# A hybrid decoder layer on one core: other orders at the first pair, the late pairs and the last scalings

## The chip, the core and the metric

The kernel runs on one core of a Trainium2 chip. Time is device time in microseconds (us) from start to end of one execution. The core has a matmul engine (TensorE, in the profile PE, its weight loads PEld), three engines for elementwise work (VectorE = DVE, ScalarE = ACT, GpSimd = POOL) and SyncE (SP), which here issues nearly all DMAs. Every engine has its own instruction stream, executed in the order in which it is written; the streams meet only at semaphores.

## What is computed

One decoder layer over 1024 tokens of width 1024, in float32: modulation vectors from `c`; RMSNorm, one input projection, two groups of four heads of chunked linear attention with decay, each head normed and gated; an output projection and a residual; RMSNorm and a squared-ReLU MLP with a residual; a last RMSNorm with gain.

```python
mod = silu(c) @ w_ada + b_ada            # shift1, scale1, gate1, shift2, scale2, gate2
h = rms_norm(x) * (1 + scale1) + shift1
# per head, chunks of 64: scores inside the chunk, a state from chunk to chunk
o = chunk_gated_linear_attention(q, k, v, log_a, 64)
o = rms_norm(o, g) * silu(gate)          # o * exp(-0.5 * ln(mean(o*o) + eps))
x = x + gate1 * (concat(o) @ w_out)
h = rms_norm(x) * (1 + scale2) + shift2
x = x + gate2 * (square(relu(h @ w_mlp1)) @ w_mlp2)
return rms_norm(x, final_norm_g)
```

## The kernel before

Every large product is made in three passes of a rounded format: both operands are split into a high part (a rounding copy, on ACT) and a low part (the rest, on POOL or DVE), and PE adds high x high, high x low and low x high. One step is a matmul of 128x128 weights with 128x512 data.

The span falls into the first norm (to 40 us), three groups of input units with attention in between (to 224 us), eight *pairs* (224 to 440 us), the output projection (to 520 us), the MLP and, after 1130 us, the last norm. The change touches the pairs and the last norm.

**A pair** makes two column blocks of the input projection as a 2x2 block product with seven instead of eight half products: P1 to P7. Their weights are quarters of `w_in` (`pair_quarter`, loaded by SP in `load_pair_quarter`) and sums of quarters, made on DVE (`weight_sum_of`, S1 to S4; S3, S2, S1 and S4 feed P7, P6, P5 and P3). ACT rounds each (`pair_high`), POOL takes the low part (`pair_low`), PE multiplies (`pair_product`, 12 matmuls; P7 in four pieces of three matmuls, `seventh_piece`, whose right operand SP loads piece by piece as `piece_x` and `piece_y`). DVE adds the products to the four quarters of the result (`join` "11", "u", "22", "21", "12"; "u" is the sum that two of them share), after ACT has saved one product (`copy_part`). Each quarter lies in a bank that a later pair writes: `c_read[...]` counts the reads that free it. The first piece of a pair's P7 waits for `c_read["12"]` of the pair before, which `silu_of` "12" raises.

Two pairs make one head: the early one its queries and forget gate, the late one its output gate and values. `paired(gi, h)` runs for gi = 3, 4, 5 and `gates(6)` last; each has a version for each engine, and for PE it is `two_pairs`. Between the products PE does the attention of the head before, in steps (`attend(n)`): transposed keys `k`, state updates `up`, scores `sc`, outputs `o`, sums of squares `ss`, transposed values `v`. ACT's `output` copies an attention output and squares it, the squares are split (`sq_hi` on ACT, `sq_lo` in DVE's `low_squares`), `ss` sums them; `norm_log` and `norm_exp` (or `read_out` in the first three groups) make the inverse root; DVE multiplies it in (`norms`). ACT loads a table before a logarithm and again before an exponential. `far_keys` and `far_queries` on DVE scale half of the keys and of the queries by a chunk's decay, for scores that span two chunks.

At the first pair (p = 0) the group H0 ends: ACT's `read_out(7, "ss")` takes two logarithms and two exponentials of a head pair, DVE's `read_out(7)` norms (`normed`) and `gate` gates head 0. `piece_y` lies where the statistics of one of these heads lie, so SP's `load_piece(0, 1)` waits for `normed`. `high_fourth` and `low_fourth` split the fourth right operand, which P4 uses.

**The end.** PE transposes tile by tile of x back (`y_bank`). ACT sums squares and takes roots, DVE inverts (`root`), multiplies by gain and root (`last_norm`) into `out_stage`; some half tiles were multiplied by the gain alone before their root was known, and get the root later (`scale_left` on ACT, a loop at the end of POOL's stream, one operation in `last_norm(7)` on DVE). SP stores tile after tile. The last add to x runs in three parts on DVE (L3180, L3183, L3187); the third waits for PE's last product.

Of the kernel before, what the change touches and what calls it, by code (L numbers as in the profile page):

```python
# [25 lines left out]
ACT = mybir.ActivationFunctionType  # L26
# [264 lines left out]
def hybrid_layer(nc, x, c, w_ada, b_ada, w_in, gate_w2, gate_b2, gla_g, lb_logits, hgrn_g, w_out, w1, w2,  # L291
# [3 lines left out]
    with ExitStack() as ctx:  # L295
# [359 lines left out]
        def _(sp):  # L655
# [57 lines left out]
            def load_piece(p, j):  # L713
# [6 lines left out]
                if p == 0 and j == 1:  # L720
                    sp.wait_ge(normed, before("ss", 3))
# [200 lines left out]
            for t in range(TT - 1):  # L922
                sp.wait_ge(read["y"], 4 + 2 * (t + 1) if t < 4 else 13 + t - 4)
                if t in (3, 4, 5):
                    sp.wait_ge(scaled_x, 2 * KT + t - 2)
                if t in (3, 6):
                    sp.wait_ge(normalised, 2 * TT + t // 3)
                sp.dma_start(out[0, t * P:(t + 1) * P, :], out_stage[:, t, :]).then_inc(stored, 16)
            for j in (1, 0):
                sp.wait_ge(read["y"], 17 - j)  # L930
                sp.dma_start(out[0, D - P:D, j * HALF:(j + 1) * HALF],
                             out_stage[:, TT - 1, j * HALF:(j + 1) * HALF]).then_inc(stored, 16)
# [4 lines left out]
        def _(pool):  # L937
# [129 lines left out]
            for t, j in ((3, 1), (4, 0), (5, 0)):  # L1067
                cols_ = slice(j * HALF, (j + 1) * HALF)
                pool.wait_ge(read["y"], 4 + 7)
                pool.wait_ge(rms_ready, 2 + t + 1)  # L1070
                pool.tensor_scalar(out_stage[:, t, cols_], out_stage[:, t, cols_], fin[:, t, 3:4], None, ALU.mult
                                   ).then_inc(scaled_x, 1)
# [3 lines left out]
        def _(act):  # L1076
# [114 lines left out]
            def group(name, gi, h):  # L1191
# [135 lines left out]
                else:  # L1327
# [6 lines left out]
                    read_out(7, "ss")  # L1334
# [17 lines left out]
            def copies(gi):  # L1352
# [16 lines left out]
                def output(half):  # L1369

                    src = bank_of("o", half)
                    act.wait_ge(normed, before("o", gi) + half)
                    act.activation(stat[:, 0, :], src, ACT.Square).then_inc(o_squared, 1)
                    act.activation(tok(mixed[:, gi + 1], half), src, ACT.Copy).then_inc(read["o"], 1)
                    act.wait_ge(o_squared, before("o", gi) + half + 1)
                    act.activation(sq_hi[:, 0, :], stat[:, 0, :], ACT.Copy).then_inc(sq_hi_ready, 1)
# [38 lines left out]
            def paired(gi, h):  # L1415
# [9 lines left out]
                if early:  # L1425
                    pair_high(early, P6)
                wait_join(act, early, 0)
                keys(0)
                if not early:
                    pair_high(early, P6)  # L1430
                copy_part(early, 0)
                if not early:
                    high_fourth()
                pair_high(early, P5)
# [319 lines left out]
            for n, (t, j) in enumerate(Y_ORDER):  # L1754
# [19 lines left out]
                if (t, j) == (3, 1):  # L1774
                    scale_left(3)
            scale_left(6)


        @block.tensor
        def _(pe):  # L1780
# [312 lines left out]
            def two_pairs(name, gi):  # L2093
# [209 lines left out]
        def _(dve):  # L2303
# [210 lines left out]
            def group(name, gi, h):  # L2514
# [71 lines left out]
                def gate(u, n, head, half=None, place=None):  # L2586


                    th, xx = (t0[:, :], t1[:, :]) if half is None else (tok(t0, place), tok(t1, place))
                    for hf in (0, 1) if half is None else (half,):  # L2590
                        dve.wait_ge(unit_read[hf], u + 1)
                    dve.scalar_tensor_tensor(th, th, 1.0, xx, ALU.add, ALU.mult).then_inc(gate_silu, 1)
                    dve.wait_ge(gate_silu, n + 1)

# [733 lines left out]
```

## Time and profile before

| what | us |
|---|---|
| median of 3 runs (1162.1 to 1164.61) | 1164.46 |
| the profiled execution, own time | 1164.09 |
| its span, first to last instruction | 1162.3 |
| PE busy in the span | 1133.2 (97%) |
| DVE busy | 865.7 (74%) |
| ACT busy | 613.0 (53%) |
| POOL busy | 496.9 (43%) |

Times below count from the start of the profiled span. Busy time of PE is modelled and overlaps from matmul to matmul; distances between starts of matmuls show its pace. The granted clock of PE has a mean of 0.993 of full speed over the span; its levels here are 1.00 (2.4 GHz) and 0.50 (1.2 GHz).

### The profile page before, as it was taken

Reading aid. Unit: us, or ns where it says so; the run is one execution under the profiler, and the core shown is the slowest. Engines: PE = TensorE matmul, PEld = TensorE weight load, DVE = VectorE, ACT = ScalarE, POOL = GpSimd, SP = SyncE. Lnnn points to the kernel's source line nnn. Section 1 sums busy time; section 2 is a strip of 40 time slices with the busy share of each in tenths; the row PEclk is TensorE's granted clock in tenths of the full one; section 3 lists DMA queues with packets and bytes.
Section 4 is the critical chain, followed back from the end, with each engine's and each line's share of the span. In section 5 each row is a group of like instructions: output and inputs, shape, how many; then the busy total and the mean of one; then the engine's idle time right before and its main releaser. Section 6 shows DMA issues by size and latency. Waiting matters only on the chain.

```text
span 1162.3 us, 15518 instructions
## 1 busy us (share of the span) xinstructions
PE 1133.2 (97%) x5483; PEld 935.7 (81%) x5483; DVE 865.7 (74%) x1033; ACT 613.0 (53%) x933; POOL 496.9 (43%) x320
## 2 busy tenths in 40 slices
PE   7999999999999999999999999999999999999996
PEld 6788788777878788888888888888888888888885
DVE  6898887778677767377976765677795875966876
ACT  7763555757566566255654555455663533524424
POOL 1021122144343345427525353344466675666741
PEclk9999999989999999999999999999999999999998
DMA  9778387344353536721455344544624637437203
GB/s 359 260 235 271 129 210 203 77 127 123 101 168 106 151 104 227 239 90 75 140 167 182 136 155 135 181 143 160 190 63 161 227 91 262 162 128 275 69 2 145
DMA packets 162948, 186.71 MB, mean 161 GB/s; under 512 B 7604, under 2 KB 119352, under 8 KB 159928
## 3 DMA queue, kind: packets, MB, share of 16 engines
q1 hardware_dynamic: 160472, 179.44, 46.6%
q0 software_dynamic: 2400, 6.29, 2.8%
q8 instruction: 44, 0.72, 0.3%
q14 instruction: 32, 0.26, 0.1%
HBM read 138.51 MB, written 40.89 MB: 154 GB/s over the span
## 4 chain that ended last, share of the span: by engine, by line
PE 89%; DVE 3%; DMA 3%; ACT 2%; issue 1%; SPq 1%; POOL 0%; DVEq 0%; ACTq 0%
PE unit_bank L1782 19%; PE unit_bank L2220 9%; PE unit_bank L2221 9%; PE unit_bank L2222 9%; PE small_bank L2220 9%; PE small_bank L2221 9%; PE small_bank L2222 9%; PE small_bank L1782 4%; PE unit_bank L2067 3%; PE unit_bank L2069 3%; PE unit_bank L2068 3%; DMA ada_slot<-in_w_ada_dram 1%; PE small_bank L1821 1%; PE small_bank L1924 1%; DVE ada_acc L2321 1%
## 5 line engine op out<-in xcount | busy, mean ns | idle before, releaser
L1026 POOL TENSOR_TENSOR wr_lo<-quarter,wr_hi 128x512 fp32r<-128x512 f32 x122 | 198.1, 1635 | 174.2 <-ACT wr_hi L1570 174.1
L2220 PE MATMUL unit_bank<-op_hi,wr_hi 128*128 128x512 f32 x452 | 176.8, 391 | 0.2 <-issue 0.2
L2222 PE MATMUL unit_bank<-op_hi,wr_lo 128*128 128x512 f32 x452 | 176.2, 390 | 0.0
L2221 PE MATMUL unit_bank<-op_lo,wr_hi 128*128 128x512 f32 x452 | 176.1, 390 | 0.0
L2220 PE MATMUL small_bank<-op_hi,wr_hi 128*128 128x512 f32 x448 | 174.7, 390 | 0.0
L2221 PE MATMUL small_bank<-op_lo,wr_hi 128*128 128x512 f32 x448 | 174.5, 389 | 0.0
L2222 PE MATMUL small_bank<-op_hi,wr_lo 128*128 128x512 f32 x448 | 174.5, 389 | 0.0
L1570 ACT ACTIVATE wr_hi<-wr_full 128x512 fp32r<-128x512 f32 x90 | 56.8, 631 | 173.3 <-DVE wr_full L2986 165.6
L1570 ACT ACTIVATE wr_hi<-quarter 128x512 fp32r<-128x512 f32 x136 | 83.0, 626 | 90.2 <-PE unit_bank L2222 51.2
L2986 DVE TENSOR_TENSOR wr_full<-quarter,quarter 128x512 f32<-128x512 f32 x90 | 89.2, 992 | 55.4 <-PE small_bank L2222 23.7
L1782 PE MATMUL unit_bank<-a_hi,w_hi 128*128 128x512 f32 x304 | 121.2, 399 | 0.0
L1782 PE MATMUL unit_bank<-a_hi,w_lo 128*128 128x512 f32 x304 | 118.6, 390 | 0.0
L1782 PE MATMUL unit_bank<-a_lo,w_hi 128*128 128x512 f32 x304 | 118.6, 390 | 0.0
L1026 POOL TENSOR_TENSOR wr_lo<-wr_full,wr_hi 128x512 fp32r<-128x512 f32 x48 | 80.5, 1679 | 76.3 <-ACT wr_hi L1570 53.6
L2220 PEld LDWEIGHTS unit_bank<-op_hi,wr_hi 128*128 128x128 f32 x452 | 84.9, 188 | 18.7 <-issue 1.2
L2222 PEld LDWEIGHTS unit_bank<-op_hi,wr_lo 128*128 128x128 f32 x452 | 84.9, 188 | 17.7
L2221 PEld LDWEIGHTS unit_bank<-op_lo,wr_hi 128*128 128x128 f32 x452 | 84.9, 188 | 17.6 <-issue 0.2
L2220 PEld LDWEIGHTS small_bank<-op_hi,wr_hi 128*128 128x128 f32 x448 | 84.1, 188 | 17.5 <-POOL wr_lo L1026 0.2
L2222 PEld LDWEIGHTS small_bank<-op_hi,wr_lo 128*128 128x128 f32 x448 | 84.1, 188 | 17.6
L2221 PEld LDWEIGHTS small_bank<-op_lo,wr_hi 128*128 128x128 f32 x448 | 84.2, 188 | 17.2
L941 POOL TENSOR_TENSOR w_lo<-raw,w_hi 128x1024 fp32r<-128x1024 f32 x11 | 29.4, 2673 | 122.5 <-ACT w_hi L1083 122.5
L983 POOL TENSOR_TENSOR pw_lo<-pair_quarter,pw_hi 128x512 fp32r<-128x512 f32 x32 | 49.2, 1538 | 58.9 <-ACT pw_hi L1344 58.9
(382 smaller groups left out, 2368.0 us busy)
## 6 DMA issues: line engine op xcount, KB each, us to landing
quarter<-in_w_mlp_dram SPq DMA_DIRECT2D x128, 256.0 KB, 4.1
hidden_scratch<-hid SPq DMA_DIRECT2D x98, 256.0 KB, 2.3
ada_slot<-in_w_ada_dram SPq DMA_DIRECT2D x48, 512.0 KB, 6.7
op_full<-hidden_scratch SPq DMA_DIRECT2D x21, 1024.0 KB, 4.8
pair_quarter<-in_w_in_dram SPq DMA_DIRECT2D x32, 256.0 KB, 4.0
piece_x<-t_scratch SPq DMA_DIRECT2D x16, 512.0 KB, 4.1
piece_y<-t_scratch SPq DMA_DIRECT2D x32, 256.0 KB, 3.5
raw<-in_w_out_dram SPq DMA_DIRECT2D x16, 512.0 KB, 4.5
```

The source lines that it names most:

```text
L941: pool.tensor_tensor(w_lo[slot][:, :, :], raw[slot][:, :, :], w_hi[slot][:, :, :].bitcast(F32), ALU.subtract).then_inc(wlo_ready, 1)
L983: pool.tensor_tensor(pw_lo[place][:, :, :], pair_source(prod), pw_hi[place][:, :, :].bitcast(F32), ALU.subtract).then_inc(pair_lo, 1)
L1026: pool.tensor_tensor(wr_lo[slot][:, :, :], split_source(n), wr_hi[slot][:, :, :].bitcast(F32), ALU.subtract).then_inc(wr_lo_pool, 1)
L1570: act.activation(wr_hi[slot][:, :, :], split_source(n), ACT.Copy).then_inc(wr_hi_ready, 1)
L1782: return pe.matmul(out_ap, left, right, start=start, stop=stop)
L2067: pe.matmul(dst, wh, hi[:, k, :], start=k == 0 and prod not in (P6, P3), stop=False, skip_group_check=True)
L2068: pe.matmul(dst, wh, lo[:, k, :], start=False, stop=False, skip_group_check=True)
L2069: mm = pe.matmul(dst, wl, hi[:, k, :], start=False, stop=k == KH - 1, skip_group_check=True)
L2220: pe.matmul(dst, wh, ah, start=opens, stop=False, skip_group_check=True)
L2221: pe.matmul(dst, wh, al, start=False, stop=False, skip_group_check=True)
L2222: mm = pe.matmul(dst, wl, ah, start=False, stop=k == KH - 1, skip_group_check=True)
L2986: dve.tensor_tensor(dst[:, :, :], a[:, :, :], b[:, :, :], op).then_inc(w_sum, 1)
```

## The change

1. **First pair.** ACT: the two logarithms (`first_logs`) come first, then P6's rounding, the keys and the part's copy, then the exponentials (`first_exps`). They take the two heads in the other order. DVE: norm and gate of H0 (`first_norms`, `first_gate`) stand behind S1, `join` "11" and `states(0)`; `masks(0)` comes before `low_fourth`. PE: the scores (`attend(2)`) come before the seventh product's pieces 1 and 2. SP's load of `piece_y` waits for the first of the two norms instead of both.
2. **Late pairs of the three heads.** DVE: S4 right behind `join` "11", `low_squares(1)` before the queries, S2 and `join` "21" before `far_keys`, `join` "12" before `norms(1)`, `far_queries` behind S1 of the next pair. ACT: `value_of(0)` and the rounding of P7 and P2 come before `norm_log(1)` and `norm_exp(1)`; `output` writes the rounded squares first, straight from the bank, and then the full ones.
3. **Gates.** `low_squares(0)` before S2.
4. **End.** DVE takes both halves of tile 3 and the left half of tile 5, ACT those of tiles 6 and 7, POOL that of tile 4 alone. SP stores tile 4 in two halves and tile 7 in one piece.

On SP:

```diff
                 if p == 0 and j == 1:
-                    sp.wait_ge(normed, before("ss", 3))
+                    sp.wait_ge(normed, before("ss", 2) + 3)
...
+            sp.wait_ge(scaled_x, 2 * KT + 2)
+            store(3)
+            sp.wait_ge(read["y"], 4 + 9)
+            store(4, right)
+            sp.wait_ge(scaled_x, 2 * KT + 3)
+            store(4, left)
+            sp.wait_ge(read["y"], 4 + 11)
+            store(5)
+            sp.wait_ge(read["y"], 4 + 12)
+            sp.wait_ge(normalised, 2 * TT + 1)
+            store(6)
+            sp.wait_ge(read["y"], 4 + 13)
+            sp.wait_ge(normalised, 2 * TT + 2)
+            store(7)
```

On POOL:

```diff
-            for t, j in ((3, 1), (4, 0), (5, 0)):
...
+            pool.wait_ge(read["y"], 4 + 7)
+            pool.wait_ge(scaled_x, 2 * KT + 2)
+            pool.wait_ge(rms_ready, 2 + 4 + 1)
+            pool.tensor_scalar(out_stage[:, 4, 0:HALF], out_stage[:, 4, 0:HALF], fin[:, 4, 3:4], None, ALU.mult
+                               ).then_inc(scaled_x, 1)
```

On ACT:

```diff
                     read_out(7, "v")
-                    read_out(7, "ss")
+            def first_logs():
+                act.wait_ge(filled["ss"], before("ss", 2) + 4)
+                for which in (1, 0):
+                    act.activation(stat[:, which, :], SB[2 + which][:, :], ACT.Ln, bias=eps, scale=1.0 / P
+                                   ).then_inc(read["ss"], 1)
+            def first_exps():
+                for n, which in enumerate((1, 0)):
+                    act.wait_ge(read["ss"], before("ss", 2) + 2 + n + 1)
+                    act.activation(stat[:, which, :], stat[:, which, :], ACT.Exp, scale=-0.5).then_inc(o_rms, 1)
...
                     act.wait_ge(normed, before("o", gi) + half)
+                    act.activation(sq_hi[:, 0, :], src, ACT.Square).then_inc(sq_hi_ready, 1)
                     act.activation(stat[:, 0, :], src, ACT.Square).then_inc(o_squared, 1)
                     act.activation(tok(mixed[:, gi + 1], half), src, ACT.Copy).then_inc(read["o"], 1)
-                    act.wait_ge(o_squared, before("o", gi) + half + 1)
-                    act.activation(sq_hi[:, 0, :], stat[:, 0, :], ACT.Copy).then_inc(sq_hi_ready, 1)
...
-                if early:
-                    pair_high(early, P6)
+                if not early:
+                    first_logs()
+                pair_high(early, P6)
                 wait_join(act, early, 0)
                 keys(0)
-                if not early:
-                    pair_high(early, P6)
                 copy_part(early, 0)
                 if not early:
+                    first_exps()
+                pair_high(early, P5)
+                if not early:
                     high_fourth()
-                pair_high(early, P5)
...
                 value_of(1, late, "22")
-                norm_log(1)
-                norm_exp(1)
                 pair_high(late + 1, P7)
                 pair_high(late + 1, P2)
                 value_of(0, late, "21")
+                norm_log(1)
+                norm_exp(1)
                 tanh_of(t0, 1, late, "12")
...
-                if (t, j) == (3, 1):
-                    scale_left(3)
             scale_left(6)
+            scale_left(7)
```

On PE:

```diff
                 pair_product(early, P6)
+                if early:
+                    seventh_piece(early, 2)
+                attend(2)
                 if not early:
                     seventh_piece(early, 1)
-                seventh_piece(early, 2)
-                attend(2)
+                    seventh_piece(early, 2)
```

On DVE:

```diff
                 def low_squares(half):
                     dve.wait_ge(sq_hi_ready, before("split", gi) + half + 1)
+                    dve.wait_ge(o_squared, before("o", gi) + half + 1)
...
                 weight_sum_of(early, "S1")
+                if early:
+                    far_queries(cum_of(gi - 1), gi - 1)
                 dve.wait_ge(decay_ready, gi)
                 join(early, "11")
                 states(0)
                 if early == 0:
+                    first_norms()
+                    first_gate()
+                    masks(0)
                     low_fourth()
-                weight_sum_of(early, "S4")
-                masks(0)
+                    weight_sum_of(early, "S4")
+                else:
+                    weight_sum_of(early, "S4")
+                    masks(0)
...
                 join(late, "11")
+                weight_sum_of(late, "S4")
...
+                low_squares(1)
                 dve.wait_ge(decay_ready, gi + 1)
...
-                low_squares(1)
...
-                weight_sum_of(late, "S4")
                 join(late, "u")
                 join(late, "22")
...
                 weight_sum_of(late + 1, "S3")
-                far_keys(gi)
                 weight_sum_of(late + 1, "S2")
                 join(late, "21")
-                far_queries(own_cum, gi)
+                far_keys(gi)
+                join(late, "12")
                 norms(1)
-                join(late, "12")
                 silu_of(t0, 1, late, "12", made + 4)
...
                 gate_quarter(t1, 0, early, "21", 4, 0, 15)
+                low_squares(0)
                 weight_sum_of(late, "S2")
-                low_squares(0)
...
                         root(3)
+                        for j in (1, 0):
+                            scale_by_root(3, j, scaled_x)
...
-                if t == 7:
...
+                if t == 5:
+                    scale_by_root(5, 0, read["y"])
```

## Rows read from the trace of the kernel before

**Rows 1.** The page's chain that ended last: share of the span by engine.
```profile
PE 89%; DVE 3%; DMA 3%; ACT 2%; issue 1%; SPq 1%; POOL 0%; DVEq 0%; ACTq 0%
```

**Rows 2.** Stretches: us, busy of PE, PEld, DVE, ACT, POOL, then PEclk, DMA.
```profile
29.50:33.00 3.50, 3.50 (x19) 3.50 (x18) 2.98 (x7) 2.81 (x6) 0.00 (x0) 0.51 1.05 403
230.90:234.30 3.40, 1.51 (x10) 0.97 (x8) 3.03 (x4) 3.40 (x6) 1.50 (x1) 1.00 0.19 37
234.40:241.10 6.70, 6.13 (x14) 4.79 (x15) 6.59 (x9) 2.31 (x4) 4.21 (x3) 0.50 0.54 174
282.10:285.50 3.40, 2.13 (x10) 1.42 (x8) 3.20 (x6) 3.39 (x6) 0.86 (x1) 1.00 0.00 0
```

**Rows 3.** PE from 230 to 247 us: start, length, what, [idle before, releaser].
```profile
232.31 1.13 PE L1782 MATMUL small_bank<-v_nat,k_nat 128*128 128x128 f32 x8 [1.03 <-issue]
234.97 0.79 PE L2067 MATMUL unit_bank<-a_hi,pw_hi 128*128 128x512 f32 x1 [1.53 <-POOL pw_lo L983]
...
246.74 0.50 PE L2087 MATMUL unit_bank<-piece_y,pw_hi 128*128 128x512 f32 x1
```

**Rows 4.** Timeline of ACT, the same stretch.
```profile
229.28 1.28 ACT L1263 ACT_TABLE_LOAD   x1
...
232.11 0.62 ACT L1344 ACTIVATE pw_hi<-pair_quarter 128x512 fp32r<-128x512 f32 x1
```

**Rows 5.** Timeline of DVE, the same stretch.
```profile
231.24 1.42 DVE L2575 SCALAR_TENSOR_TENSOR mixed<-mixed,cols,stat 128x512 f32<-128x512 f32 x2 [2.76 <-ACT stat L1263]
...
237.12 1.48 DVE L2760 SCALAR_TENSOR_TENSOR state<-state,decay_tile,small_bank 128x128 f32<-128x128 f32 x4
```

**Rows 6.** Timeline of SP's DMA issues, the same stretch.
```profile
232.68 0.81 SPq L726 DMA_DIRECT2D piece_y<-t_scratch  x2
233.53 0.43 SPq L728 DMA_DIRECT2D piece_x<-t_scratch  x1
...
241.58 0.79 SPq L726 DMA_DIRECT2D piece_y<-t_scratch  x2
```

**Rows 7.** Loads of `piece_y` issued from 232 to 234 us.
```profile
DMA to landing us min/median/max: 3.0/3.3/3.6
```

**Rows 8.** The load of `piece_x` issued at 233.5 us.
```profile
DMA to landing us min/median/max: 4.8/4.8/4.8
```

**Rows 9.** Timeline of PE at the first late pair's end, 283 to 287 us.
```profile
283.61 0.39 PE L2068 MATMUL unit_bank<-a_lo,pw_hi 128*128 128x512 f32 x1
283.84 0.39 PE L2069 MATMUL unit_bank<-a_hi,pw_lo 128*128 128x512 f32 x1
285.65 1.06 PE L1821 MATMUL small_bank<-ident,vT 128*128 128x128 f32 x8 [1.42 <-ACT vT L1413]
286.83 0.47 PE L2087 MATMUL unit_bank<-piece_x,pw_hi 128*128 128x512 f32 x1
```

**Rows 10.** Timeline of ACT at the same late pair.
```profile
278.92 0.63 ACT L1344 ACTIVATE pw_hi<-pair_quarter 128x512 fp32r<-128x512 f32 x1 [1.91 <-DMA pair_quarter<-in_w_in_dram]
...
285.41 0.60 ACT L1403 ACTIVATE t<-unit_bank 128x512 f32<-128x512 f32 x1
```

**Rows 11.** Timeline of DVE at the same late pair.
```profile
270.93 0.69 DVE L2728 TENSOR_TENSOR unit_bank<-unit_bank,k_nat 128x512 f32<-128x512 f32 x1
...
275.11 0.68 DVE L2701 TENSOR_TENSOR pw_full<-pair_quarter,pair_quarter 128x512 f32<-128x512 f32 x1
...
286.04 0.69 DVE L2734 SCALAR_TENSOR_TENSOR t<-t,unit_bank 128x512 f32<-128x512 f32 x1 [0.67 <-ACT t L1403]
```

**Rows 12.** Timeline of SP's DMA issues at the same late pair.
```profile
272.67 0.50 SPq L728 DMA_DIRECT2D piece_x<-t_scratch  x1
```

**Rows 13.** PE's waits from 260 to 440 us: total us, times, longest.
```profile
PE small_bank L1782 <- DVE sq_lo L2767: 2.1, 6, 1.0
```

**Rows 14.** Timeline of SP, 1143 us to the end.
```profile
1157.28 1.88 SPq L931 DMA_DIRECT2D out_dram<-out_stage  x2
```

**Rows 15.** DMA traffic from 1156.3 to 1163 us, 40 slices of 0.17 us.
```profile
GB/s 416 391 25 0 49 147 391 416 416 416 416 416 440 392 391 440 465 440 391 391 318 404 403 404 391 404 440 416 208 25 12 0 0 0 0 0 0 0 0 0
```

More of the change, by code:

```diff
@@ L920, in _, with store @@
                         load_x_again(4 * (g - UP_GROUPS - 1) + n)
[L922 to L932, printed above, removed]
+            def store(t, cols_=slice(0, D)):
+                sp.dma_start(out[0, t * P:(t + 1) * P, cols_], out_stage[:, t, cols_]).then_inc(stored, 16)
+            left, right = slice(0, HALF), slice(HALF, D)
+            for t in range(3):
+                sp.wait_ge(read["y"], 4 + 2 * (t + 1))
+                store(t)
+            sp.wait_ge(scaled_x, 2 * KT + 2)
[12 more added lines that the diff above has]
+            store(7)
             sp.wait_ge(stored, 16 * (TT + 1))
@@ L1066, in _ @@
                     hidden_sums(n - 2)
-            for t, j in ((3, 1), (4, 0), (5, 0)):
[L1068 to L1072, printed above, removed]
+            pool.wait_ge(read["y"], 4 + 7)
[3 more added lines that the diff above has]
+                               ).then_inc(scaled_x, 1)
         @block.scalar
@@ L2584, in both_read @@
                         dve.wait_ge(unit_read[half], u + 1)
[L2586 to L2593, printed above, removed]
-                    dve.wait_ge(normed, before("ss", gi) + (half + 1 if half is not None and head == 7 else 0))
-                    dst = row(mixed, head) if half is None else tok(row(mixed, head), half)
-                    dve.scalar_tensor_tensor(dst, th, 0.5, dst, ALU.mult, ALU.mult).then_inc(gated, 1)
                 u0 = 4 * gi + 1
@@ L2676, in group, with first_norms, first_gate @@
                     far_queries(q_cum, gi)
-                read_out(7)
+                if own == "P":
+                    read_out(7)
                 if name == "P0":
                     then(dve.memset(masked[:, :, :], 0.0))
-                if own == "H":
-                    gate(u0 + 3, hh, hh)
+            def first_norms():
+                for n, which in enumerate((1, 0)):
+                    dve.wait_ge(o_rms, before("ss", 2) + 2 + n + 1)
+                    dst = tok(mixed[:, 2 + which], 1)
+                    dve.scalar_tensor_tensor(dst, dst, cols[:, R_GG:R_GG + 1], stat[:, which, :], ALU.mult, ALU.mult
+                                             ).then_inc(normed, 1)
+            def first_gate():
+                for half in range(2):
+                    dve.wait_ge(unit_read[half], 13)
+                dve.scalar_tensor_tensor(t0[:, :], t0[:, :], 1.0, t1[:, :], ALU.add, ALU.mult).then_inc(gate_silu, 1)
+                dve.wait_ge(gate_silu, 1)
+                dve.wait_ge(normed, before("ss", 2))
+                dve.scalar_tensor_tensor(mixed[:, 0], t0[:, :], 0.5, mixed[:, 0], ALU.mult, ALU.mult).then_inc(gated, 1)
             def weight_sum_of(p, kind):
@@ L2874, in gates @@
                 weight_sum_of(early, "S1")
+                far_queries(cum_of(gi - 1), gi - 1)
                 dve.wait_ge(decay_ready, gi)
@@ L3264, in root, with scale_by_root @@
                 dve.reciprocal(fin[:, t, 3:4], fin[:, t, 3:4]).then_inc(rms_ready, 1)
+            def scale_by_root(t, j, sem_):
+                cols_ = slice(j * HALF, (j + 1) * HALF)
+                dve.wait_ge(rms_ready, 2 + t + 1)
+                dve.wait_ge(read["y"], 4 + 8)
+                dve.tensor_scalar(out_stage[:, t, cols_], out_stage[:, t, cols_], fin[:, t, 3:4], None, ALU.mult
+                                  ).then_inc(sem_, 1)
             def fourth_tile():
@@ L3282, in last_norm @@
                                              ALU.mult, ALU.mult).then_inc(read["y"], 1)
-                if t == 7:
-                    dve.wait_ge(read["y"], Y_ORDER.index((t, 0)) + 1)
-                    dve.tensor_scalar(out_stage[:, t, 0:HALF], out_stage[:, t, 0:HALF], fin[:, t, 3:4], None, ALU.mult
-                                      ).then_inc(read["y"], 1)
+                if t == 5:
+                    scale_by_root(5, 0, read["y"])
             for n in range(PRODUCTS - 1):
```

## The prediction

> **What bounds the kernel now.** I read the page's chain of waits first: TensorE (PE) holds 89% of it [rows 1]. A change that adds no matmul can save time only where PE stands still, where its clock is low, and after its last matmul. So I went through the timeline of PE for every step longer than the normal one. The normal step between two 128x512 matmuls is 0.23 us (the first two of [rows 9]). From 90 us on there are few places: the first pair at 231 to 247 us, the end of each late pair (three times, 53 us apart), one wait in the group with the gates at 417 us, and the tail. These are the places that the edits touch.
>
> At the first pair PE waits 1.03 us before the state updates and 1.53 us for POOL's low part of P6 [rows 3]. The cause is ACT: after the two logarithms it loads a table, makes both exponentials, and only then copies the keys and rounds P6 [rows 4]. Behind this stop the granted clock is 0.50, the lower of its two levels, for 6.7 us [rows 2]: PE loses another 3.4 us. In the 3.4 us before the fall PE had worked only 1.51 us.
>
> At a late pair PE stops 1.42 us for `vT`, which ACT copies late, and the seventh product starts at 286.83, just after DVE's `silu_of` "12" (286.04 + 0.69) [rows 9, 11]. That product writes the bank which `silu_of` frees (`c_read["12"]`). Over 260 to 440 us PE also waited 2.1 us for the squares' low part [rows 13].
>
> **First pair, part by part.** Time stands on ACT at 229.28, when both logarithms are done [rows 4]. Now come the rounding of P6 (0.62, to 229.9), the keys (to 230.4), the part's copy (to 231.0), then the table load (1.28, to 232.3) and the first exponential (to 232.9). The keys are there before PE ends P2 (its last matmul ended at 232.31 - 1.03 = 231.3, so the next can start at 231.1), and the updates start there and end at 232.25 (1.13) [rows 3]. P6 before: rounded at 232.73, PE began at 234.97, so 2.2 us; now 229.9 + 2.2 = 232.1. PE runs on: P6, twelve matmuls, 232.2 to 234.9. The two waits are gone and with them, I expect, the fall of the clock. The scores (1.65 us) now come here: to 236.5.
>
> Then something else is late. The second seventh piece needs `piece_y`, and SP holds its load until the first head is normed. On DVE the norm now stands behind S1, `join` "11" and the four state updates (1.48), which wait for PE: 232.35 to 233.85, norm to 234.6 [rows 5]. Before it was done at 232.0 and SP issued at 232.68 [rows 5, 6]. Now SP issues `piece_y` at 234.6 and 235.0 and behind them `piece_x` at 235.4; the loads take up to 3.6 and 4.8 us [rows 7, 8]: 238.6 and 240.2. PE waits 2.1 us, makes piece 1, waits 0.9 us, makes piece 2 and P5 (0.7 + 2.7): 243.7. Piece 3's load goes out when piece 1 is done (239.4); before, it went out at 241.58 and PE used it at 246.74, 5.16 us later, while the scores covered part of it [rows 3, 6]. Now 239.4 + 5.0 = 244.4. Against 246.74 that is **2.4 us gained**. With loads at their fastest row (3.0 and under 4.8) it would be 4.0, with every load at 4.8 it is 1.0. DVE's gate, `masks(0)` and `low_fourth` end by 242.5, ahead of their use.
>
> **Late pairs.** `output` rounds the squares first, so `low_squares` starts after two reads of PSUM instead of three operations, 0.5 us earlier; this starts the chain that runs over forget, logarithm, scan and exponentials to the end of the late pair. S4 moves up behind `join` "11", which now ends at 271.1 (270.93 + 0.69 - 0.5): from 275.11 to 271.1 [rows 11]. With it SP's loads of the next pair's quarters come right behind `piece_x` (272.67 [rows 12], now 272.2), at 272.7. They queue behind its 512 KB and land at 276.3 at the earliest (3.6 us after issue, as the slower `piece_y` [rows 7]) and 277.6 at the latest (272.2 + 4.8 [rows 8] + 0.6 for their own 256 KB at the pace of [rows 15]); I take 277.0, where ACT before waited 1.91 us and rounded P1 at 278.92 [rows 10]. P1 is low at 279.0, S2 follows at 279.7, `join` "21" at 280.4, `value_of(0)` at 281.0. So `vT` is ready when PE ends P1 at 282.3, not at 285.65. The three waits for `sq_lo`, P3 and P1 shrink too.
>
> But the logarithm and the exponential, which `value_of(0)` overtakes, now stand between it and the tanh: 281.0 + 1.28 + 0.7 + 1.28 + 0.6 + 0.6 = 285.5, with the table loads of [rows 4] and the 128x512 operations of [rows 4, 10] (ACT's tanh before: 285.41 to 286.01 [rows 10]). DVE's norm (to 285.7) and `silu_of` "12" follow: 286.4 to 286.5. The seventh product starts 286.5 instead of 286.83. The stop has moved from the `vT` transposes to the seventh product; PE now stands about 3.1 us in one piece (283.4 to 286.5), right behind 1.06 us of small transposes. **Gain 0.33 us each, 1.0 us in all.** Bounds: nothing, if the quarters land as late as they did relative to issue (ACT in series is then as long as before), and 0.7 each, if DVE alone sets it. `far_queries` goes into the time in which DVE waits for P2 of the next pair, and costs nothing; its reader, the scores, stands behind P2, P6 and a seventh piece. Without that cover it would be 1.1 us (0.4 and 0.7).
>
> **Gates.** `low_squares(0)` ahead of S2 and the earlier rounding: of the longest `sq_lo` wait (1.0 [rows 13]) 0.6 goes, one DVE operation. Bounds 0 and 1.2 (the whole step).
>
> **Tail.** DVE takes both halves of tile 3 (0.5 each) into its wait for PE, ACT loses one scaling there and gets tile 7's, POOL keeps one. DVE's last norm ends at 1156.8, ACT's last scaling too, and the last store goes out at 1156.9 instead of 1158.0 [rows 14]. The stores are already limited by what the DMA engines move: about 410 GB/s without a hole from 1157.3 to 1161.0 [rows 15], so 512 KB take 1.26 us. The left half of tile 4 flows from 1155.8, then tiles 5, 6, 7: 1155.8 + 0.63 + 3 x 1.26 = 1160.2, and before, by the same sum, 1161.4. **Gain 1.2 us**; bounds 0.6 (issue order loses half a tile) and 2.0 (no queue). The Trainium skill (SBUF — State Buffer, The DMA setup-cost knee) speaks against one whole last store: about 2 us fixed plus bytes at 436 GB/s, an estimate of 3.2 us for 512 KB against 2.6 for the half that is last now. With it the last landing would be 1156.9 + 3.2 = 1160.1, so queue and rule agree here within 0.1 us.
>
> **Sum.** 2.4 + 1.0 + 0.6 + 1.2 = 5.2 us off the profiled execution's 1164.1 (span 1162.3, and 1.8 around it), which lies 0.4 below the median of the runs, 1164.46: 1158.9.
>
> **What the clock does.** The fall at the first pair came after PE had worked 1.51 of 3.4 us [rows 2]. The late stops of before, 2.13 of 3.4 us, left it at 1.00. The new late stop holds 1.06 us of transposes and 3.1 us of nothing: it lies beyond the row that fell. How it falls against whatever the chip looks at I can't say, so I give each of the three stops one chance in three to bring the clock down. A fall costs half of the time at the lower level: rows show 6.7 us (3.4 lost) and 3.4 us (1.7 lost) [rows 2]; I take 2.5. PE is the chain for 20 us behind that stop, so all of it counts. The Trainium skill (TensorE: Matmul & The Clock Gate, HAM oscillation — how this bites in real kernels) tells of a kernel whose waits between bursts drop the clock each time; by that all three stops would pay, 3 x 2.5 = 7.5 us, and the time would be 1166.4. It leads to case D.
>
> **The rivals and their times.** Case B is the forecast; the others are its rivals.
>
> A, the terms add up and the clock holds: 1158.9, chance 0.35.
>
> B, the same with one fall in the three late stops: 1158.9 + 2.5 = **1161.4**, from 1160.6 to 1162.3; chance 0.41. The likeliest.
>
> C, two falls, or one and the first pair's kept: 1163.9, chance 0.14. For it: the first pair still has 3.0 us of stops between 236.5 and 240.2. Against: matmuls stand between them.
>
> D, the other side: every gathered stop drops the clock, each for 6.7 us: 1158.9 + 3 x 3.4 = 1169.1; it is slower from two such falls and one shorter on. Chance 0.05.
>
> E, the change doesn't do what it says: loads decide the first pair as before and the late chain keeps its length; the tail alone stays: 1162.9, chance 0.05.
>
> A change of 0.2% (2.3 us, bounds 1162.1 and 1166.8) is about what a measurement of this kernel tells from none. Faster: A, two thirds of B, little of C: 0.67. Same: the rest of B, most of C, E: 0.26. Slower: D and some of C: 0.07. The range goes from A's better half to the upper end of C: 1157.9 to 1164.3; B's own is 1160.6 to 1162.3.
>
> **What would show it.** In the profile after: no wait of PE before the updates and P6 at 231 to 235 us; the clock at 1.00 there; piece 1 waiting for a DMA near 236.5 to 238.6; the seventh piece 3 near 244.4. At each late pair no wait at `vT`, and one stop of about 3 us before the seventh product's first matmul, ended by DVE's `silu_of`. A clock row of 0.50 behind one of them is case B. The last store issued near 1156.9 less what was saved before. Wrong it would be if the seventh product started well ahead of 286.5, if `piece_y` came late by other loads, or if the clock held or fell each time.

## The result

The kernel after takes 1176.19 us (median of 4 runs, 1171.46 to 1176.48) against 1163.31 beside it: 1.0104 times the time of before, interval 1.0086 to 1.0123, so 1.0% slower. The prediction said 1161.4 and faster. The profiled execution of after is the shortest of the four: 1171.46, its span 1169.7 against 1162.3, so 7.4 us more; the other three took 4.7 to 5.0 us more than it, at a mean granted clock of 0.985 to 0.987 instead of 0.991.

The chain of waits of the page, as [rows 1]: PE's share falls, "issue" and DVE grow.

```profile
PE 87%; DVE 5%; issue 4%; DMA 1%; ACT 1%; SPq 1%; DVEq 0%; ACTq 0%
```

Windows of after (columns as in [rows 2]): the first pair, then stretches at the three *late stops*. By a late stop I mean the time for which PE stands still at the end of a late pair, before the first matmul of the next pair's seventh product.

```profile
230.90:234.30 3.40, 3.40 (x20) 2.96 (x20) 2.87 (x7) 3.39 (x5) 0.73 (x2) 1.00 0.02 5
234.40:241.10 6.70, 4.32 (x28) 3.30 (x27) 6.67 (x5) 1.96 (x3) 3.12 (x2) 1.00 0.74 229
...
281.60:285.00 3.40, 0.00 (x0) 0.00 (x0) 2.18 (x5) 3.37 (x7) 0.00 (x0) 1.00 0.00 0
285.00:288.40 3.40, 3.35 (x10) 2.79 (x11) 3.37 (x4) 1.33 (x4) 1.79 (x1) 0.50 0.16 42
...
343.10:346.50 3.40, 3.40 (x10) 2.63 (x9) 1.98 (x2) 1.60 (x3) 2.38 (x2) 0.51 0.71 214
...
397.70:404.50 6.80, 6.06 (x16) 4.87 (x17) 4.05 (x6) 2.84 (x6) 3.07 (x2) 0.50 0.38 115
```

At the first pair the clock is 1.00 in this execution where it was 0.50 for 6.7 us [rows 2]. But PE does nothing at all from 281.6 to 285.0, and then the clock is at its lower level for 3.4 us; the same at the second pair, and for 6.8 us at the third. Before, no such fall stood behind a late pair.

PE at the first pair and at the first late stop, as [rows 3] and [rows 9]:

```profile
230.94 1.05 PE L1802 MATMUL small_bank<-v_nat,k_nat 128*128 128x128 f32 x8
...
234.56 1.05 PE L1802 MATMUL small_bank<-q_rel,k_rel 128*128 128x128 f32 x8
...
238.21 0.50 PE L2107 MATMUL unit_bank<-piece_y,pw_hi 128*128 128x512 f32 x1 [1.99 <-DMA piece_y<-t_scratch]
...
239.56 0.50 PE L2107 MATMUL unit_bank<-piece_x,pw_hi 128*128 128x512 f32 x1 [0.39 <-DMA piece_x<-t_scratch]
...
243.08 0.48 PE L2107 MATMUL unit_bank<-piece_y,pw_hi 128*128 128x512 f32 x1
```

```profile
274.63 0.47 PE L2087 MATMUL unit_bank<-a_hi,pw_hi 128*128 128x512 f32 x1 [1.18 <-DVE unit_bank L2753]
...
280.51 1.04 PE L1841 MATMUL small_bank<-ident,vT 128*128 128x128 f32 x8
285.05 0.76 PE L2107 MATMUL unit_bank<-piece_x,pw_hi 128*128 128x512 f32 x1 [3.50 <-issue]
```

The other engines at the late stop, as [rows 10] and [rows 11]: ACT, then DVE, then POOL.

```profile
275.37 0.63 ACT L1365 ACTIVATE pw_hi<-pair_quarter 128x512 fp32r<-128x512 f32 x1 [1.66 <-DMA pair_quarter<-in_w_in_dram]
...
279.02 0.60 ACT L1433 ACTIVATE vT<-unit_bank 128x512 f32<-128x512 f32 x1 [1.38 <-DVE unit_bank L2753]
279.64 1.28 ACT L1400 ACT_TABLE_LOAD   x1
...
281.64 1.28 ACT L1405 ACT_TABLE_LOAD   x1
...
283.47 0.58 ACT L1423 ACTIVATE t<-unit_bank 128x512 f32<-128x512 f32 x1
```

```profile
267.24 0.69 DVE L2753 TENSOR_TENSOR unit_bank<-unit_bank,k_nat 128x512 f32<-128x512 f32 x1
267.84 1.18 DVE L2726 TENSOR_TENSOR pw_full<-pair_quarter,pair_quarter 128x512 f32<-128x512 f32 x1
...
270.96 2.12 DVE L2879 SCALAR_TENSOR_TENSOR q_rel<-q_rel,t 128x1024 f32<-128x1024 f32 x1
...
284.27 0.68 DVE L2759 SCALAR_TENSOR_TENSOR t<-t,unit_bank 128x512 f32<-128x512 f32 x1
```

```profile
269.82 2.17 POOL L993 TENSOR_TENSOR pw_lo<-pw_full,pw_hi 128x512 fp32r<-128x512 f32 x1 [1.35 <-ACT pw_hi L1365]
```

What loads of `pair_quarter` took from issue to landing, the two that S4 releases: after (issued from 269.5 to 270.5 us), and the same two before (275.7 to 276.6).

```profile
DMA to landing us min/median/max: 5.7/5.9/6.0
```

```profile
DMA to landing us min/median/max: 3.0/3.1/3.2
```

To place the 7.4 us I matched the matmuls of both traces and followed the difference of their starts, after minus before. The first matmul of the squares' sum, before and after:

```profile
274.20 0.47 PE L1782 MATMUL small_bank<-sq_hi,ones 128*128 128x512 f32 x1 [0.23 <-DVE sq_lo L2767]
```

```profile
270.12 0.39 PE L1802 MATMUL small_bank<-sq_hi,ones 128*128 128x512 f32 x1
```

The difference is -3.3 us at P5 of the first pair (243.66 before, 240.36 after) and -4.1 at the squares' sum at 274.20 (270.12). The seventh product of the next pair, 286.83 before, starts at 285.05: -1.8. So the first late stop costs 2.3 us, and the lower clock behind it 1.7 more: about -0.1. At the second, 339.99 became 341.74 (+1.8) and some 3.3 behind the clock; at the third, 393.26 became 398.44 (+5.2) and +8.0. The gates give 0.6 back, the MLP loses 0.8 at 1087 us, and the tail from PE's last matmul to the end is 8.47 instead of 9.44 us: +7.4. All that was gained and more went in the three late stops and the lower clock behind them: 12 us. Counted from the squares' sum to the seventh product, the three late ends take 14.9, 14.0 and 14.8 us, where they took 12.6, 12.4 and 12.5: 6.2 us in all are wait.

### The profile page after: what moved, and what is told of

Same layout as the page of the kernel before. It is cut to its first block, busy times and chain, and to the rows that moved or that the text cites. A ratio compares the mean times of both kernels' runs of the same rounds, so it can differ in the third digit from the quotient of the medians.

```text
span 1169.7 us, 15525 instructions
## 1 busy us (share of the span) xinstructions
PE 1134.0 (97%) x5483; PEld 938.0 (80%) x5483; DVE 877.8 (75%) x1035; ACT 613.0 (52%) x933; POOL 495.1 (42%) x318
## 4 chain that ended last, share of the span: by engine, by line
PE 87%; DVE 5%; issue 4%; DMA 1%; ACT 1%; SPq 1%; DVEq 0%; ACTq 0%
PE unit_bank L1802 19%; PE unit_bank L2242 9%; PE unit_bank L2244 9%; PE unit_bank L2243 9%; PE small_bank L2242 9%; PE small_bank L2244 9%; PE small_bank L2243 9%; PE small_bank L1802 3%; PE unit_bank L2087 3%; PE unit_bank L2088 2%; PE unit_bank L2089 2%; PE small_bank L1841 1%; DVE ada_acc L2343 1%; DMA ada_slot<-in_w_ada_dram 1%; PE small_bank L1944 1%
```

## The experiments

All times are medians; each ratio is to the kernel before, run beside it on the same chip.

**late_only.** The kernel before with the late part alone (DVE's and ACT's order in `paired`, the order in `output`, `far_queries`):

```diff
-                norm_log(1)
-                norm_exp(1)
                 pair_high(late + 1, P7)
                 pair_high(late + 1, P2)
                 value_of(0, late, "21")
+                norm_log(1)
+                norm_exp(1)
                 tanh_of(t0, 1, late, "12")
...
                 join(late, "11")
+                weight_sum_of(late, "S4")
```

> The kernel before with the late pairs' part alone (order of sums, joins, far keys, far queries and squares; the value copy ahead of the norm). Theory 1, the late pairs alone carry the loss: in the trace after, TensorE stands against before at -4.1 us ahead of the first late stop and at +7.6 us behind the third, 11.7 us lost, so 1163.3 + 11.7 = 1175.0 or more, with the granted clock at 0.50 behind each of the three late stops. Theory 2, the loss needs the earlier start that the first pair gives (loads that now collide): at most 1167, and stops under 2.5 us.

1176.11, ratio 1.0111 (1.0093 to 1.0129): all of the loss. The late stop is 3.5 us long at each pair, and the windows behind the three show the clock:

```profile
288.80:292.20 3.40, 3.40 (x11) 2.72 (x10) 2.21 (x3) 1.60 (x3) 2.48 (x2) 0.50 0.68 202
343.40:350.20 6.80, 5.65 (x15) 4.55 (x16) 4.45 (x6) 3.24 (x7) 3.06 (x2) 0.50 0.37 113
401.40:408.20 6.80, 5.70 (x16) 4.56 (x17) 4.39 (x6) 3.19 (x7) 3.06 (x2) 0.50 0.38 111
```

**late_back.** The kernel after with DVE's and ACT's order in `paired` (and `far_queries`) as before, the reverse of that diff; `output`, gates, first pair and end stay changed.

> The kernel after with the late pairs' order on ScalarE and VectorE as before; first pair, squares, gates and end stay changed. Theory 1: what is left is the gain of 4.1 us up to 270 us, 1.0 at the end, and 0.8 lost in the MLP: 1163.3 - 4.3 = 1159.0, clock 1.00 from 231 to 425 us, seventh product behind the transposes of vT with a stop of about 0.4 us. Theory 2, first pair, gates or end carry part of the loss: 1164 or more.

1162.37, ratio 0.9997 (0.9987 to 1.0007). The late stops are those of before (1.4 us at `vT`), the clock stays at 1.00 there. But the time is not 1159: theory 1 has the right place and leaves out 3 us. One window of its trace shows where, behind the wait for `piece_y`:

```profile
235.60:239.00 3.40, 1.38 (x11) 0.85 (x10) 3.37 (x3) 0.65 (x2) 2.18 (x1) 1.00 0.96 321
239.00:242.40 3.40, 3.10 (x8) 2.44 (x8) 3.40 (x4) 0.00 (x0) 0.00 (x0) 0.50 0.75 201
```

The wait is as long as in after's own trace (2.0 us), where the clock held. Its ten runs spread from 1159.93 to 1164.02.

**first_only.** The kernel before with the first pair's part alone.

> The kernel before with the first pair's part alone. By the trace of late_back TensorE gains 3.3 us up to 238 us and loses 1.1 to 1.7 of it when the clock falls behind the wait for piece_y; the fall of before, 3.4 us, is among what is gained. If that fall comes in most runs: 1163.0 - 2.2 = 1160.8, if for 6.8 us: 1162.5. The forecast said 2.4 gained: 1160.6. Rival, nothing: 1163.

1162.91, ratio 0.9994 (0.9981 to 1.0008), runs from 1161.02 to 1166.09. In the profiled execution, which kept its clock, PE was 3.0 us ahead at P5; over ten runs no gain is to be seen, which was the rival's 1163.

**back_filled.** late_back, with the first pair's scores made twice, which fills the wait for `piece_y`:

```diff
+                        if gi == FIRST_PAIRED and (p[0], p[2]) == ("sc", 0):
+                            scores(prev, both, gi, False)
                         {"sc": scores, "up": updates, "o": outputs}[p[0]](prev, both, gi)
```

> The kernel with the late pairs as before, first pair and end as after, and the first pair's scores made twice (same values), which fills 1.65 of the 2.0 us for which TensorE waits for piece_y. Theory: the fall of the clock behind this wait (3.4 us at 239.0 in the profile of late_back, 6.8 us in that of filled_stop) eats the gain of the first pair; held up, the runs lie 1.7 to 3.4 us below those of late_back (1162.4): 1159.0 to 1160.7. Rival, the first pair's stop doesn't set the clock, or the gain is lost otherwise: 1162 or more.

1159.22, ratio 0.9963 (0.9951 to 0.9976), and the nine runs lie within 1158.88 to 1160.53. PE does more work and the kernel is 3.2 us faster than late_back (4.0 by the two ratios). The same windows:

```profile
235.60:239.00 3.40, 2.89 (x27) 2.31 (x25) 3.37 (x4) 0.57 (x2) 2.21 (x1) 1.00 0.92 294
239.00:242.40 3.40, 2.43 (x11) 1.82 (x11) 3.40 (x4) 0.00 (x0) 0.00 (x0) 1.00 0.72 205
```

**filled_stop.** The kernel after, with the last four `vT` transposes repeated:

```diff
-                    mm = turn([vT[which][:, t * P:(t + 1) * P] for t in range(4 * half, 4 * half + 4)], b)
+                    for _ in range(6 if u0 is None and half else 1):
+                        mm = turn([vT[which][:, t * P:(t + 1) * P] for t in range(4 * half, 4 * half + 4)], b)
```

> The kernel after, with the last four transposes of vT at each late pair made six times over (the same values), so that TensorE works through 2.6 of the 3.5 us in which it waits; what it waits for is unchanged. Theory 1a, the clock takes more than half of the loss: it stays at 1.00 behind the three stops, the stops end where they ended, and 1.7 + 1.7 + 3.4 us come back from the profiled 1171.5: 1164.7, in the runs at 1176 more. Theory 1b, the waits take the loss and the clock falls for another reason: 1171 or more and the falls still there.

1168.52, ratio 1.0042 (1.0026 to 1.0057): 7.7 us less than after (7.2 by the two ratios). PE still waits 1.5 us. The seventh product starts 14.8, 14.7 and 14.8 us behind its pair's squares (after: 14.9, 14.0 and 14.8), so what it waits for has not become faster; but behind all three stops the clock is at 1.00:

```profile
285.26 3.22 PE L1841 MATMUL small_bank<-ident,vT 128*128 128x128 f32 x28
289.97 0.47 PE L2108 MATMUL unit_bank<-piece_x,pw_hi 128*128 128x512 f32 x1 [1.49 <-issue]
```

```profile
290.00:293.40 3.40, 3.40 (x17) 2.83 (x18) 3.32 (x4) 2.06 (x4) 2.09 (x2) 1.00 0.37 88
345.10:348.50 3.40, 3.40 (x17) 2.83 (x18) 3.33 (x4) 2.07 (x4) 2.09 (x2) 1.00 0.36 84
400.20:407.00 6.80, 6.79 (x36) 5.79 (x37) 5.04 (x8) 3.34 (x6) 4.48 (x3) 1.00 0.50 146
```

So, by these medians, more than half of the 12.9 us are the clock's (theory 1a); some 5 are the waits' own, net of what the end gains. The expected 1164.7 took the first pair's clock for held; here it fell at 240 for 6.8 us.

**norm_before_value.** The kernel after with ACT's `norm_log(1)`, `norm_exp(1)` back ahead of P7, P2 and `value_of(0)`, and no other change.

> The kernel after with one thing undone: ScalarE makes the norm's logarithm and exponential ahead of P7, P2 and the value copy, as before. Theory 1, the gathered stop alone brings the clock down: the stop is split again (about 1.6 us at the transposes, the seventh product at 283.4 instead of 285.05), the clock stays up behind the three late stops: 1171.5 - 4.8 - 6.8 = 1159.9, runs to 1164. Rival, the order on VectorE (S4 early, the late join of the last quarter) carries the loss: 1168 or more.

1161.56, ratio 0.9988 (0.9971 to 1.0005). Two instructions and two table loads in another place are worth some 14 us. ACT now makes the norm in the time in which, in after, it waited 1.38 us for DVE's `join` "21" (its `vT` at 279.02), so the seventh product starts 13.0, 13.2 and 12.9 us behind the squares: 4.6 us less wait in all. PE's stop is 1.3 to 1.6 us and lies ahead of the transposes, and the clock stays at 1.00 behind all three; the other 9 us or so are left for the clock by subtraction, which is argued and not measured here.

```profile
286.45 1.06 PE L1841 MATMUL small_bank<-ident,vT 128*128 128x128 f32 x8 [1.33 <-ACT vT L1433]
287.62 0.47 PE L2107 MATMUL unit_bank<-piece_x,pw_hi 128*128 128x512 f32 x1
```

**quarters_first.** The kernel after with SP's loads in another order:

```diff
-                    load_piece(p + 1, 0)
                     load_pair_quarter(p + 1, 0)
                     load_pair_quarter(p + 1, 1)
+                    load_piece(p + 1, 0)
```

> The kernel after, with the loads of the next pair's first two quarters issued ahead of piece_x and not behind it. Theory 3, the stop is long because these quarters queue behind 512 KB of piece_x: they land 3.0 to 3.6 us after their issue (before they took 3.0 and 3.25) instead of 5.7 and 6.0, near 272.9 instead of 275.3, the seventh product starts up to 2.3 us sooner and the stop is 1.2 to 1.6 us; with the clock held 1171.5 - 6.9 - 6.8 = 1157.8, with the falls kept 1164.6. Rival, the chain behind the landing is held by VectorE or by the DMA engines' load whatever the order: 1171 or more.

1169.52, ratio 1.0058 (1.0043 to 1.0073). P1's quarter now lands 3.3 us after its issue at 272.7, so the queue behind `piece_x` was what held it (the second quarter, issued at 273.2, takes 4.7). But the stop is still 2.9 us and the clock falls behind two of three. ACT rounds P1 without waiting for a DMA, right behind a tanh that waits for DVE's `q_rel`; the chain had a second limit just behind the first.

```profile
276.73 0.60 ACT L1423 ACTIVATE t<-unit_bank 128x512 f32<-128x512 f32 x1 [3.37 <-DVE q_rel L2879]
277.22 0.62 ACT L1365 ACTIVATE pw_hi<-pair_quarter 128x512 fp32r<-128x512 f32 x1
```

```profile
287.76 0.47 PE L2107 MATMUL unit_bank<-piece_x,pw_hi 128*128 128x512 f32 x1 [2.93 <-issue]
```

**s4_late.** The kernel after with the late S4 where before had it, ahead of `join` "u".

> The kernel after with S4 of the late pair where the kernel before had it. Theory 4: moving S4 up gained nothing, because the quarters then queue behind piece_x and land no earlier (in the trace after at 275.3, which with the 4.1 us by which the pair began earlier answers to 279.4; before 278.8), and cost the wait of 1.34 us ahead of P3, because POOL's low part of P3 then runs beside VectorE's q_rel (2.12 us instead of 1.22; POOL 2.17 instead of 1.29). So here the wait ahead of P3 goes (under 0.5), the quarters take 3.0 to 3.3 us and land at most as late, the seventh product starts 0.3 to 0.8 sooner for each pair; falls of the clock stay: 1176.2 - 1.5 = 1174.7. By the forecast's theory (early S4 brings early landings) it is 1178 or more, and the stop over 4.5 us.

1172.77, ratio 1.0088 (1.0070 to 1.0106), whose interval overlaps that of after. The two quarters, issued 2.6 us later against the pair (273.20 less 0.98, by which this trace runs behind that of after, against 269.58), land 0.2 us sooner: in 2.9 to 3.1 us. Moving S4 up brought nothing forward. The landing, DVE and PE of this run:

```profile
DMA to landing us min/median/max: 2.9/3.0/3.1
```

```profile
271.35 1.23 DVE L2878 SCALAR_TENSOR_TENSOR q_rel<-q_rel,t 128x1024 f32<-128x1024 f32 x1
```

```profile
275.30 0.50 PE L2087 MATMUL unit_bank<-a_hi,pw_hi 128*128 128x512 f32 x1 [0.86 <-POOL pw_lo L993]
...
285.65 0.47 PE L2107 MATMUL unit_bank<-piece_x,pw_hi 128*128 128x512 f32 x1 [3.54 <-issue]
```

`q_rel` takes 1.23 us again. The wait ahead of P3 shrinks only from 1.18 to 0.86, since it is now POOL that is late; my "under 0.5" missed. The forecast's theory (1178 or more) falls.

**tanh_first.** The kernel after, the last quarter first on both engines:

```diff
                 value_of(0, late, "21")
+                tanh_of(t0, 1, late, "12")
                 norm_log(1)
                 norm_exp(1)
-                tanh_of(t0, 1, late, "12")
...
                 join(late, "21")
-                far_keys(gi)
                 join(late, "12")
-                norms(1)
                 silu_of(t0, 1, late, "12", made + 4)
+                far_keys(gi)
+                norms(1)
```

> The kernel after, with the last quarter's join, tanh and silu of each late pair ahead of the norm's logarithm and exponential on ScalarE, and ahead of far keys and norm on VectorE. Theory 1, the stop is long because two table loads, a logarithm and an exponential (3.9 us) stand between the value copy and the tanh: join at 279.7, tanh 280.3, silu 281.0 on the time line of after, so the seventh product follows the transposes at once (281.7); far keys then end near 283.9 instead of 281.8 and the transposes of the keys start there, not at 286.47: 2.6 us less at each pair, and no fall of the clock since the stop is 1.3 us: 1171.5 - 7.7 - 6.8 = 1157.0, runs 1157 to 1161. Rival, VectorE's work as a whole is the bound and far keys, norm and gate come back as a wait for the keys or for P6: 1166 or more.

1166.78, ratio 1.0033 (1.0017 to 1.0050). The seventh product follows the transposes at once (283.07), but a stop of 2.9 to 3.1 us stands behind it: the key transposes want the bank that ACT frees with the copies of `v_nat`, and these stand behind the norm. Neither theory named this one; VectorE had ended far keys 3 us before.

```profile
286.96 0.92 PE L1841 MATMUL small_bank<-ident,k_end 128*128 128x128 f32 x4 [2.95 <-ACT v_nat L1388]
```

```profile
282.01 1.28 ACT L1400 ACT_TABLE_LOAD   x1
...
285.84 1.07 ACT L1388 ACTIVATE v_nat<-small_bank 128x512 f32<-128x512 f32 x2
```

**norm_later.** tanh_first with the norm moved on into the next pair:

```diff
                 tanh_of(t0, 1, late, "12")
-                norm_log(1)
-                norm_exp(1)
...
                 copy_part(early, 0)
+                if early:
+                    copies(gi - 1)[3](1)
+                    copies(gi - 1)[4](1)
```

(In `copies(gi - 1)`, `[3]` and `[4]` are `norm_log` and `norm_exp` of the group before; DVE's `norms(1)` goes behind `states(0)`.)

> As tanh_first, and the norm's logarithm and exponential go into the next pair on ScalarE, behind the copies of v_nat, P6, the keys and the part's copy; VectorE's norm goes behind the next state updates. Theory 1: in tanh_first the stop of 3.1 to 3.3 us was left only because both v_nat copies, which free the bank for the key transposes, stood behind the norm. Now these copies end near 284.4 and far keys at 283.9 (time line of tanh_first): the key transposes start near 284.2 instead of 286.96, no stop over 1 us, the clock holds behind all three: 1166.8 - 3 x 2.7 - 1.7 = 1157.0. Rival: there is more work on ScalarE and VectorE than fits, and the wait comes back later (P6, P5 or the updates): 1163 or more.

1155.77, ratio 0.9951 (0.9937 to 0.9965). The stop is gone at all three pairs of its trace, and so is the fall of the clock there. PE's waits from 260 to 440 us:

```profile
PE unit_bank L2091 <- DVE unit_bank L2757: 3.2, 3, 1.2
...
PE small_bank L1845 <- DVE k_end L2530: 0.5, 2, 0.2
```

**norm_later_s4.** norm_later with S4 late and the first scores made twice.

> norm_later with S4 of the late pair where the kernel before had it, and the first pair's scores made twice. If both theories hold the terms add: 1157.0 - 3 x 1.3 (no wait ahead of P3) - 2.0 (the clock held behind piece_y) = 1151.1; if the chain from the quarters' landing is what is left, 1155 to 1157; if the wait comes back later, 1160 or more.

**1154.00, ratio 0.9930 (0.9913 to 0.9947)**: the best, 8.2 us below the kernel before beside it (1162.22). The terms didn't add up to 1151.1: the late S4 leaves the wait ahead of P3 to POOL, as in s4_late.

```profile
PE unit_bank L2094 <- POOL pw_lo L993: 2.6, 3, 0.9
```

**joins_first.** norm_later_s4 with S4, `join` "u" and "22" of the late pair ahead of `q_rel`.

> norm_later_s4 with S4 and the joins u and 22 of the late pair ahead of q_rel on VectorE. What is left there at each late pair is a wait of 1.02 us ahead of P3, which waits for join 22 (274.6) and POOL's low part (275.2, on the time line of s4_late). Theory: q_rel (1.23) is not needed as early as these joins; with them first P3 starts up to 1.0 sooner, the seventh product then hangs on the chain from the quarters' landing, so 0.5 to 1.0 us less for each pair: 1151.0 to 1152.5. Rival: tanh and silu 11, which wait for q_rel, come 1.3 late and hold up P2 of the next pair by as much: 1154 or more.

1156.36, ratio 0.9946 (0.9932 to 0.9959), whose interval overlaps that of norm_later_s4: no gain, where 1151.0 to 1152.5 was expected. P3's waits fell from 2.6 to 0.8 us in all, and three others came in their place (all waits from 260 to 440 us: 3.4 us became 3.7).

## Why the prediction was wrong

The forecast, 1161.4, is 14.8 us short. By the traces and runs above some 7 us of that are the late waits (6.2 lost, 1.0 gained by the forecast), some 5 the clock behind them (7.2 to 7.7 against 2.5) and 2.4 the first pair; 0.8 in the MLP and 0.2 at the tail are small. These parts come from different kernels and need not add up exactly. "On the time line of before" below means that PE's lead, 4.1 us at 270 us, is added.

**First pair: the mechanism right, the clock wrong.** The waits for the updates and P6 went; `piece_y` was issued at 234.22 (forecast 234.6) and PE started on it at 238.21 (238.6), on `piece_x` at 239.56 (240.2). Piece 3 came at 243.08, not 244.4, since its loads took 2.9 to 3.4 us, not 5.0: gain 3.7 instead of 2.4. But "with them, I expect, the fall of the clock" failed. Nine kernels here have the first pair's order of after: behind the new wait for `piece_y` the clock fell in the profiled execution of seven, for 3.4 or 6.8 us, and held in after's and first_only's. In the three with the wait filled it held. first_only measured what is left of the gain: nothing that its ten runs could show.

**Late pairs, the chain: the term that failed was the landing.** The step "with it SP's loads of the next pair's quarters come right behind `piece_x` ... I take 277.0" asked how long 256 KB take behind 512 KB, at the end of one load. The loads took 5.7 to 6.0 us, landing at 275.28, which answers to 279.4 on the time line of before: 2.4 us later than taken, and half a microsecond later than with S4 in its old place (278.8). Of the 2.4 us 1.4 are the load itself (5.7 us from the issue at 269.58, where 4.3 was taken), the rest its issue: `join` "11" started at 267.24, which answers to 271.3 and not to 270.4, so the half microsecond that the squares should give had not reached it. From there the forecast's chain was right: 9.45 us from landing to `silu_of`'s end was said, 9.67 measured. So the stop is 3.5 to 3.7 us and not 3.1, and the three late pairs lost 2.3, 1.6 and 2.3 us where I had 0.33 gained at each. My lower bound, "nothing, if the quarters land as late as they did relative to issue", was no bound: it left out that they could land later, and that the tanh's place behind two table loads would then be paid in full.

**An effect that the forecast left out.** S4's move also moved POOL's low part of P3 to 269.82, beside DVE's work on `cum` and `q_rel`. In each of the seven traces with S4 early and `q_rel` behind it, `q_rel` takes 2.12 or 2.13 us at all three pairs; in each of the six with S4 late and that order, 1.22 or 1.23. The part of P3 takes POOL 2.17 instead of 1.29. Both operations before:

```profile
273.98 1.22 DVE L2845 SCALAR_TENSOR_TENSOR q_rel<-q_rel,t 128x1024 f32<-128x1024 f32 x1
```

```profile
276.60 1.29 POOL L983 TENSOR_TENSOR pw_lo<-pw_full,pw_hi 128x512 fp32r<-128x512 f32 x1 [4.43 <-ACT pw_hi L1344]
```

The Trainium skill (SBUF — State Buffer, SBUF: two separate sides) says that a VectorE operation with two inputs in SBUF and a GpSimd operation that reads SBUF lock each other out for a whole instruction. The trace agrees: POOL ends at 271.99, and `q_rel` ends 1.09 us after that. With it `join` "22" is late and PE waits 1.18 us ahead of P3, where it waited 0.28 and I had said that this wait shrinks. But this wait costs little by itself: the landing sets the seventh product, which in s4_late starts 14.5 us behind the squares at all three pairs (after: 14.9, 14.0 and 14.8).

**The clock: the rival that I gave 0.05 was the case.** I gave each gathered stop one chance in three. The windows show it behind three of three in after, late_only and s4_late, behind two of three in quarters_first (2.9 us idle) and one of three in tanh_first (2.9 to 3.1), and behind none in the kernels where the longest idle time there was under 1.8 us. The one row with a fall behind it had 1.51 of 3.4 us worked, and the prediction says itself that the new stop lies beyond it; the new stretch has 0.00 of 3.4, and nothing in the rows of before spoke for its holding. So the chance of one in three had no row behind it. Its price was right: 2.5 us for each fall, against 7.2 to 7.7 us for three in filled_stop. Case D is right in kind and not in length: in the profile of after two falls last 3.4 us and one 6.8, where it had 6.7 for each. The Trainium skill (TensorE: Matmul & The Clock Gate, HAM oscillation — how this bites in real kernels) tells of waits that drop the clock each time, which I had set beside the sum as 1166.4. The traces agree at all nine stops of 3.5 to 3.7 us; of the six stops of 2.9 to 3.1 us only three dropped it.

**Gates and tail.** 0.6 forecast, 0.6 measured (the wait for `sq_lo` 0.4 instead of 1.0). 1.2 forecast for the tail, 0.9 to 1.0 measured in the traces with the new end; the last store went out 3.7 us behind PE's last matmul instead of 5.1, but took 4.3 us to land, where the forecast's sum had 3.3 (the two halves before: 3.9 and 4.0).

**Left open.** A wait of PE near 1087 us with no releaser that the profile shows: 1.2 us in the trace of after, 0.7 to 0.8 in late_only, quarters_first and s4_late, at most 0.3 in the others. And why the clock holds behind the same first-pair wait in some executions.

## What to carry to other kernels

Don't gather waits: moving work so that short waits of TensorE become one long one costs the clock on top of the wait, and a repeat of harmless matmuls inside a stop that can't be removed is a cheap test of that (7.7 and 3.2 us here). When a load is issued earlier, ask what is ahead of it in the queue, and price its landing and not only its issue. And when a long operation is moved, ask which wait it filled where it stood: the norm had stood in a wait of ACT. Where PE waits for a bank, look for what frees it: the long norm belonged behind the copies that PE waited for, not ahead of them.

## What I had not expected of the hardware

Two 256 KB loads right behind one of 512 KB took 5.7 and 6.0 us, and 2.9 and 3.1 when issued 2.6 us later against the pair: by my alignment the later issue landed 0.2 us sooner. And more work made the kernel faster: sixteen extra small matmuls for 3.2 us at one place.
